# A two-layer hybrid trunk on one core: the transposes of v are asked for one projection later, and the delta branch's z projections are made beside the block inversion and parked in DRAM

## The chip, the cores and the metric

The kernel is written for one core of a Trainium2 chip. The core has four compute engines that run side by side, each through an instruction stream of its own: TensorE (PE: matmuls and transposes, results in PSUM banks), VectorE (DVE), ScalarE (ACT: activations and copies) and GpSimd (POOL). SyncE (SP) issues DMA transfers, and here so does ACT. The engines meet at semaphores. The metric is the device time of one execution in microseconds, lower is better; the time before is the median of three runs.

## What is computed

Two layers of a trunk over 512 latent tokens and 256 context tokens of width 1024. Each layer normalizes and modulates its input (shift, scale and gate come from a projection of a conditioning vector, the "ada" product), projects it by `w_in`, runs three branches of width 512 and merges them by gates:

```python
h = rms_norm(x, norm_g) * (1.0 + scale) + shift          # shift, scale, gate: silu(c) @ w_ada + b_ada
conv_val, conv_glu, conv_z, dq, dk, dv, dz, dbeta, ddecay, aq, ak, av, az, mgate = split(h @ w_in)
# delta branch: short convolution and silu of q, k, v; q and k l2-normalized; beta, g from dbeta, ddecay
sol = triangular_solve(a, rhs)                            # a = strict(k_beta k^T * decay) + I, per chunk
S   = S * exp(g_last) + (k * exp(g_last - g))^T v_new     # scan over chunks, forward and backward
y_delta = rms_norm(o_forward + o_backward, dn_norm_g) * silu(dz)
# conv branch: depthwise convolution over 31 tokens of val * sigmoid(glu), layer norm, silu, * silu(z)
# attention branch: difference of two softmaxes, 4 heads, keys over latent and context tokens, * silu(az)
x = x + gate * (sum over branches of sigmoid(mgate) * (y @ w_branch)) @ w_out
```

The first layer carries 768 tokens through everything (`TOK`); the second needs only 512 (`SEQ`) wherever the context's result is not read again.

## The kernel before

**Weights and products.** A weight unit is 128 x 1024 floats, 512 KB. It is streamed by an SP DMA into one of four `raw` buffers, ACT copies it to its rounded high part `wH` (L751), POOL subtracts to get the low part `wL` (L1676), and PE's `dense` (L418) makes three passes (high x high, low x high, high x low): 48 matmuls for 768 tokens, 24 for 512. `ahead(u)` prepares weights up to three units on. An "ada" unit is different work on the same stream: 16 small matmuls (L509) and a few tiny DVE operations (L1219, L1222).

**The order of work.** `schedule()` writes one list of items by hand, `ITEMS`, and every engine walks that list and does its own part of each item in order. Nothing is reordered at run time: an engine that waits inside one item holds back its part of all later ones. PSUM is handed out in four slots in rotation (`product`).

**The delta branch.** For each of four heads there are three projections, items `dqkv` of kind dk, dv and dq. On each, ACT copies the product into a padded tile (`pad`, L883), DVE makes the short convolution (L1356), ACT applies silu (L896, L897). In the dv item PE then transposes silu's result `vb` (`vturn`, by `turn`, L442) and ACT copies it to `Vtm` (L901); this is all inside the item dv. After it the item `dsum` of the previous head makes the sums of squares on PE (L434), from which ACT computes a reciprocal root in four steps (Ln and Exp, a table load before each, L757 and L760). After the heads come the projections val, glu of the conv branch (`glu` items) and `leaf` items, in which DVE eliminates 32 x 32 blocks (L1422, L1426), then the block inversion: `five`, `fiveb`, `six`, `sixb`, short PE steps with copies by DVE and ACT between them. Then the `scan` over chunks, and `dout` for each head: the z projection (unit dz), POOL's squares `dosq` (L1758), their sum on PE, ACT's silu of z (L1014) and reciprocal root, and DVE's `don` (L1525) and `y32` (L1532). While these run, and long after, DVE makes the 31 taps of the conv branch (L1270, L1274), a few of them at a time; `merge_steps(l, 1)` is the merge of that delta branch (its gates and its output projections).

**Ada units.** Layer 0's list holds 32 ada units that are not needed at once. Twelve (`early`) stand around the inversion of layer 0, three before `five`, three before `fiveb`, three before `six`, three before `sixb`. The other twenty (`late`) are woven at even distances into `mid`, the items of attention and of the merges in layer 0.

## Time and profile before

| | |
|---|---|
| median of three runs | 2379.46 us (2377.32 to 2382.97) |
| the profiled execution: own time | 2383.71 us |
| its span, first to last instruction | 2381.9 us |
| mean granted TensorE clock | 0.887 of full speed |
| busy: PE, DVE, ACT, POOL | 1942.8, 1073.2, 982.3, 818.1 us |

The trace is of the one profiled execution. The shares are averages over stages that have different limits, so a stage is read by itself: which engine is busy through it, and what the others wait for. The stages lie as follows in the span. Layer 0: heads of the delta branch 106 to 288 us, glu and leaf 288 to 388, inversion 388 to 442, scan to 501, dout to 568, the conv phase to about 700, attention 701 to 1203 (first head to 948), merge to 1318. Layer 1: heads 1425 to 1598, leaf 1633 to 1682, inversion 1682 to 1703, scan to 1752, dout and the conv phase to 1894, attention and the end from there.

### The profile page before, as it was taken

What the parts mean: (1) busy time and instruction counts of PE and PEld (TensorE: products, weight loads), DVE (VectorE), ACT (ScalarE), POOL (GpSimd) and SP (SyncE); (2) the same over time, 40 slices, a digit from 0 to 9 for tenths busy, and PEclk for the clock granted to TensorE, in tenths of its full rate; (3) what the DMA queues carried; (4) which work ended last, traced back from release to release, by engine and by line L of the source; (5) the groups of instructions that cost most, each with busy time, mean ns of one, the idle gap of its engine ahead of it and who ended that gap; (6) DMA issues with size and microseconds to landing.
All of it is one profiled execution on the core that took longest, in us unless ns stands there. A gap on an engine that the chain in (4) does not pass through costs nothing. (4 is left out here: it accounts for less than half of the span.)

```text
span 2381.9 us, 28536 instructions
## 1 busy us (share of the span) xinstructions
PE 1942.8 (82%) x11444; PEld 1620.6 (68%) x11444; DVE 1073.2 (45%) x1592; ACT 982.3 (41%) x1318; POOL 818.1 (34%) x428
## 2 busy tenths in 40 slices
PE   7677896999779998878789867676688599888697
PEld 6666785987658887666577746565677387666476
DVE  3444656459960232423401234557769803334302
ACT  4345542243124344544532144564343245455521
POOL 0122323544534534232134211233245454322152
PEclk8588995899889999988899888898799799999898
DMA  4221221411101221111112312122112122101023
GB/s 173 73 76 55 68 84 63 136 51 60 47 27 63 71 71 54 54 36 45 36 53 97 113 47 72 58 72 75 44 65 80 35 83 69 62 27 33 30 82 113
DMA packets 66195, 157.95 MB, mean 66 GB/s; under 512 B 5329, under 2 KB 28177, under 8 KB 65809
## 3 DMA queue, kind: packets, MB, share of 16 engines
q1 hardware_dynamic: 33264, 122.46, 15.9%
q10 hardware_dynamic: 32800, 33.66, 4.4%
q8 instruction: 93, 1.52, 0.3%
q14 instruction: 38, 0.30, 0.0%
HBM read 145.52 MB, written 10.58 MB: 66 GB/s over the span
## 5 line engine op out<-in xcount | busy, mean ns | idle before, releaser
L1676 POOL TENSOR_TENSOR wL<-raw,wH 128x1024 fp32r<-128x1024 f32 x210 | 565.0, 2693 | 1123.0 <-ACT wH L751 1122.8
L418 PE MATMUL banks<-hH,wH 128*128 128x512 f32 x1984 | 598.3, 363 | 75.3 <-issue 32.9
L418 PE MATMUL banks<-hL,wH 128*128 128x512 f32 x1984 | 583.0, 356 | 0.0
L418 PE MATMUL banks<-hH,wL 128*128 128x512 f32 x1984 | 581.1, 355 | 0.0
L418 PEld LDWEIGHTS banks<-hH,wH 128*128 128x128 f32 x1984 | 328.4, 192 | 140.3 <-issue 74.7
L751 ACT ACTIVATE wH<-raw 128x1024 fp32r<-128x1024 f32 x226 | 237.4, 1053 | 396.7 <-DMA raw<-wstream 396.4
L418 PEld LDWEIGHTS banks<-hL,wH 128*128 128x128 f32 x1984 | 327.1, 192 | 56.6 <-issue 3.4
L418 PEld LDWEIGHTS banks<-hH,wL 128*128 128x128 f32 x1984 | 326.1, 192 | 55.0
L1274 DVE SCALAR_TENSOR_TENSOR acc<-padc,vecs,acc 128x783 f32<-128x783 f32 (+1 forms) x240 | 263.8, 1170 | 0.0
L418 PE MATMUL banks<-yH,wH 128*128 128x512 f32 (+1 forms) x288 | 94.8, 384 | 51.5 <-DVE mT L1565 19.2
L509 PE MATMUL banks<-wH,csx 128*128 128x128 f32 x384 | 122.2, 343 | 13.1 <-DVE wL L1209 13.0
L1565 DVE TENSOR_TENSOR gm<-banks,sg 128x768 f32<-128x768 f32 (+1 forms) x32 | 26.4, 825 | 210.9 <-PE banks L418 147.1
L774 ACT ACTIVATE Pa<-banks,stat 128x768 f32<-128x768 f32 (+1 forms) x80 | 64.5, 811 | 137.0 <-DVE stat L1235 136.7
L509 PE MATMUL banks<-wL,csx 128*128 128x128 f32 x384 | 120.2, 338 | 0.0
L1039 ACT ACTIVATE sg<-banks 128x768 f32<-128x768 f32 (+1 forms) x48 | 33.8, 705 | 198.0 <-DVE mT L1565 115.3
L509 PEld LDWEIGHTS banks<-wH,csx 128*128 128x128 f32 x384 | 97.0, 253 | 16.1 <-issue 14.9
L509 PEld LDWEIGHTS banks<-wL,csx 128*128 128x128 f32 x384 | 97.9, 255 | 0.3 <-issue 0.2
L418 PEld LDWEIGHTS banks<-yH,wH 128*128 128x128 f32 x288 | 51.2, 203 | 64.0 <-issue 35.4
L418 PE MATMUL banks<-yL,wH 128*128 128x512 f32 (+1 forms) x288 | 91.5, 373 | 0.0
L418 PE MATMUL banks<-yH,wL 128*128 128x512 f32 (+1 forms) x288 | 91.0, 371 | 0.0
L757 ACT ACT_TABLE_LOAD x52 | 66.7, 1283 | 56.3 <-PE banks L434 55.4
L465 PE MATMUL banks<-kh,qh 64*128 64x256 f32 (+1 forms) x288 | 64.2, 564 | 30.8 <-ACT vr L1152 19.9
(249 smaller groups left out, 2607.0 us busy)
## 6 DMA issues: line engine op xcount, KB each, us to landing
raw<-wstream SPq DMA_DIRECT2D x226, 512.0 KB, 3.5
E<-g_rows ACTq DMA_DIRECT2D x16, 384.0 KB, 6.9
egb<-eg_rows ACTq DMA_DIRECT2D x20, 256.0 KB, 4.0
inb<-intra_rows ACTq DMA_DIRECT2D x20, 256.0 KB, 4.2
xs<-xT SPq DMA_DIRECT2D x1, 3072.0 KB, 16.1
intra_rows<-E ACTq DMA_DIRECT2D x8, 384.0 KB, 3.3
xs<-xT ACTq DMA_DIRECT2D x1, 3072.0 KB, 10.6
x_between<-xs ACTq DMA_DIRECT2D x8, 384.0 KB, 3.4
```

The lines of the kernel that those rows point to most:

```text
L418: last = pe.matmul(out[:, a:b], w, m[:, kt, a:b], start=(kt == 0 and j == 0), stop=(kt == kts - 1 and j == 2))
L465: last = pe.matmul(outs[m][:, o:o + b - a], q_[r, qt * P:(qt + 1) * P], k_[r, a:b], start=True, stop=True)
L509: last = pe.matmul(out[:, 0:P], csx[:, 4 * kt:4 * kt + P], w[i][:, kt * P:(kt + 1) * P], start=(kt == 0 and j == 0), stop=(kt == KT - 1 an ...
L751: act.activation(wH[w % RING][:, :], raw[w % RING][:, :], ACT.Copy).then_inc(*tick("act", "hi", v))
L757: ins = act.activation(dst[:, 0:n], place[readkey][:, 0:n], ACT.Ln, bias=e, scale=scale)
L774: act.activation(Pa[i][m][:, 0:w], place[key][:, 0:w], ACT.Exp, bias=stat[:, i, 2 + m:3 + m], accum_out=stat[:, i, 4 + m:5 + m]).then_inc( ...
L1039: act.activation(sg[d % 2][:, 0:n], place[u][:, 0:n], ACT.Sigmoid).then_inc(*tick_read("act", u))
L1274: ins = dve.scalar_tensor_tensor(acc[:, t, 0:W], padc[:, t, k:k + W], w, acc[:, t, 0:W], ALU.mult, ALU.add)
L1565: dve.tensor_tensor(dst, place[(u, j)][:, 0:n], sg[j][:, 0:n], ALU.mult).then_inc(*tick_read("dve", (u, j)))
L1676: pool.tensor_tensor(wL[w % RING][:, :], raw[w % RING][:, :], wH[w % RING][:, :].bitcast(F32), ALU.subtract).then_inc(*tick("pool", "lo", v))
```

## The change

Four things are done.

1. `vturn` and ACT's copy to `Vtm` leave the item dv and become an item of their own, `vt`, which stands after the next head's dk projection (for the last head, after the first glu item).
2. The z projections leave `dout` and become items `dz`: head 0's before the last leaf item, head 1's between `five` and `fiveb`, head 2's between `fiveb` and `six`, head 3's between `six` and `sixb`. ACT applies silu into `gl[h % 2]` and issues a DMA to a DRAM tensor `zscr`; in `dout` a DMA `z_in` brings each back, and DVE's `y32` waits for it instead of for the silu. ACT and DVE wait for the last two of the writes before the scan begins.
3. All 32 ada units of layer 0 are now `late`, woven into `mid`; none stands around the inversion.
4. Two gate projections of the delta branch's merge move up, between `dout` 0 and 1 and between 1 and 2. Semaphores are made only if they are used.

```diff
--- before.py
+++ after.py
@@ -97,7 +97,7 @@
             out.append(("dqkv", l, h, "dk"))
-            out += [("dsq", l, h - 1)] * (h > 0)
+            out += [("vt", l, h - 1), ("dsq", l, h - 1)] * (h > 0)
             out.append(("dqkv", l, h, "dv"))
@@ -106,14 +106,14 @@
         late = [("ada", 0, m) for m in range(16, 24)] + [("ada", 1, m) for m in range(24)] if l == 0 else []
-        early, late = late[:12], late[12:]
-        out += [("dsq", l, NT - 1), glu[0], ("dsum", l, NT - 1), glu[1], ("dturn", l, NT - 1), ("kq", l, NT - 1)]
-        out += leaf[:3] + [glu[2]] + leaf[3:6] + [glu[3]] + leaf[6:]
-        out += early[:3] + [("five", l)] + early[3:6] + [("fiveb", l)] + early[6:9]
-        out += [("six", l, 1), ("six", l, 0)] + early[9:] + [("sixb", l, 1), ("sixb", l, 0)]
+        dz = [("dz", l, h) for h in range(NT)]
+        out += [("dsq", l, NT - 1), glu[0], ("vt", l, NT - 1), ("dsum", l, NT - 1), glu[1], ("dturn", l, NT - 1),
+                ("kq", l, NT - 1)]
+        out += leaf[:3] + [glu[2]] + leaf[3:6] + [glu[3]] + leaf[6:7] + [dz[0]] + leaf[7:]
+        out += [("five", l), dz[1], ("fiveb", l), dz[2], ("six", l, 1), ("six", l, 0), dz[3], ("sixb", l, 1), ("sixb", l, 0)]
         out += [("scan", l, s) for s in range(NC)]
-        out += [("dout", l, h) for h in range(NT)]
-        out += merge_steps(l, 1)
+        out += [("dout", l, 0), ("gate", l, 1, 0), ("dout", l, 1), ("gate", l, 1, 1), ("dout", l, 2), ("dout", l, 3)]
+        out += merge_steps(l, 1)[2:]
         out += [("ln", l)]
@@ -142,7 +142,7 @@
         return [("av", l, item[2])]
-    if k == "dout":
+    if k == "dz":
         return [("dz", l, item[2])]
@@ -188,9 +188,11 @@
         names += ["w_high", "w_low_pool", "w_low_dve", "raw0", "raw1", "raw2", "raw3", "small_in", "x_in", "x_out", "rope_in"]
-        names += ["g_out", "eg_out", "e_in0", "e_in1", "i_out0", "i_out1"]
+        names += ["g_out", "eg_out", "e_in0", "e_in1", "i_out0", "i_out1", "z_out0", "z_out1", "z_in0", "z_in1"]
         names += ["%s_in%d%d" % (n, d, i) for n in ("eg", "intra") for d in range(2) for i in range(2)]
-        sem = {n: ctx.enter_context(nc.semaphore(n)) for n in names}
+        used = {n for n, _ in steps.values()} or {names[0]}
+        made = {n: ctx.enter_context(nc.semaphore(n)) for n in names if n in used}
+        sem = {n: made.get(n, next(iter(made.values()))) for n in names}
         count = {n: 0 for n in sem}
@@ -534,8 +537,9 @@
                     unit((kind, l, h), kind)
-                    if kind == "dv":
-                        turn(("vturn", l, h), vb[h % 2], TOK, ("silu", "dv", l, h))
+                elif k == "vt":
+                    h = it[2]
+                    turn(("vturn", l, h), vb[h % 2], TOK, ("silu", "dv", l, h))
                 elif k == "dsum":
@@ -646,10 +650,11 @@
                             last.then_inc(*tick("pe", "pe", ("O", l, s, d)))
+                elif k == "dz":
+                    unit(("dz", l, it[2]), "dz")
                 elif k == "dout":
                     n = ntok(l, "dz")
-                    unit(("dz", l, h), "dz")
                     allsum(it, ones[:, :], lambda t, a, b: do[h % 2][:, a:b], n, lambda t: ("dosq", l, h), 1)
@@ -779,6 +784,11 @@
                         *tick("e_in%d" % (h % 2), "Ein", l, h, d, by=16))
+
+            def z_in(l, h):
+
+                n = ntok(l, "dz")
+                act.dma_start(do[4 + h % 2][:, 0:n], zscr[:, h, 0:n]).then_inc(*tick("z_in%d" % (h % 2), "zin", l, h, by=16))
@@ -895,11 +905,12 @@
                     act.activation(dst[:, 0:SEQ], c3[i][:, 0:SEQ], ACT.Silu).then_inc(*tick("act", "silu", kind, l, h))
-                    if kind == "dv":
-                        key = ("vturn", l, h)
-                        act.wait_ge(*done("pe", key))
-                        act.activation(Vtm[:, :, h, :], place[key][:, 0:TOK].rearrange("p (c e) -> p c e", c=NC),
-                                            ACT.Copy).then_inc(*tick_read("act", key))
+                elif k == "vt":
+                    h = it[2]
+                    key = ("vturn", l, h)
+                    act.wait_ge(*done("pe", key))
+                    act.activation(Vtm[:, :, h, :], place[key][:, 0:TOK].rearrange("p (c e) -> p c e", c=NC),
+                                   ACT.Copy).then_inc(*tick_read("act", key))
                 elif k == "dsum":
@@ -982,6 +993,8 @@
                     if g == 0:
+                        act.wait_ge(*done("zout", l, 2))
+                        act.wait_ge(*done("zout", l, 3))
                         scan_in(l, 0)
@@ -998,20 +1011,30 @@
                         scan_in(l, s + 2)
-                elif k == "dout":
+                elif k == "dz":
                     h = it[2]
                     act.wait_ge(*done("pe", u))
-                    act.wait_ge(*done("S", l, NC, 1))
+                    act.wait_ge(*(done("zout", l, h - 2) if h >= 2 else done("glu", l, 2 + h)))
+                    act.activation(gl[h % 2][:, 0:n], place[u][:, 0:n], ACT.Silu).then_inc(*tick_read("act", u))
+                    act.wait_ge(*done("read", u, 0))
+                    act.dma_start(zscr[:, h, 0:n], gl[h % 2][:, 0:n]).then_inc(*tick("z_out%d" % (h % 2), "zout", l, h, by=16))
+                elif k == "dout":
+                    h = it[2]
+                    n = ntok(l, "dz")
                     if h == 0:
+                        act.wait_ge(*done("S", l, NC, 1))
                         act.wait_ge(*done("oT", l, NC - 1, 0))
                         act.dma_start(cs[:, :, :], rope).then_inc(*tick("rope_in", "rope_in", l, by=16))
-                    if h >= 2:
-                        act.wait_ge(*done("y32", 1, l, h - 2))
-                    act.activation(do[4 + h % 2][:, 0:n], place[u][:, 0:n], ACT.Silu).then_inc(*tick_read("act", u))
+                        z_in(l, 0)
+                        z_in(l, 1)
+                    else:
+                        act.wait_ge(*done("y32", 1, l, h - 1))
+                        if h + 1 < NT:
+                            z_in(l, h + 1)
                     rsqrt(None, do[2 + h % 2], 1.0 / P, eps, ("dors", l, h), it, n)
@@ -1480,6 +1503,9 @@
                         dve.wait_ge(*done("negeg", l))
+                        if s == 0:
+                            dve.wait_ge(*done("zout", l, 2))
+                            dve.wait_ge(*done("zout", l, 3))
                         if s:
@@ -1525,7 +1551,7 @@
                     dve.wait_ge(*done("don", l, h))
-                    dve.wait_ge(*done("read", ("dz", l, h), 0))
+                    dve.wait_ge(*done("zin", l, h))
                     if h >= 2:
@@ -1756,8 +1782,9 @@
                     pool.tensor_tensor(do[h % 2][:, 0:n], oT[:, h, 0:n], oT[:, h, 0:n], ALU.mult).then_inc(*tick("pool", "dosq", l, h))
+                    lowy(1, l, h, n, do[6 + h % 2])
+                elif k == "dz":
                     ahead(units_of(it)[0])
-                    lowy(1, l, h, n, do[6 + h % 2])
                 elif k == "glu":
```

**Place 1, ACT, the third head's v in layer 0.** `vb` is silu's result, `Vtm` its transposed copy, `rsd` the reciprocal roots of the head before, `kT` silu of k, `pad` the next product's copy. Before:

```order
L884 ACTIVATE pad_1_92<-banks 128x512
L896 ACTIVATE vb_95<-c_1_94 128x256
L897 ACTIVATE vb_95<-c_1_94 128x512
L901 ACTIVATE Vtm<-banks 128x6x128
L757 ACT_TABLE_LOAD
L757 ACTIVATE rsd_99<-banks,misc 128x768
L760 ACT_TABLE_LOAD
L760 ACTIVATE rsd_99<-rsd_99 128x768
```

After (L901 is now L912, L757 is L762, L751 is L756):

```order
L906 ACT_TABLE_LOAD
L906 ACTIVATE kT<-c_0_93 128x256
L907 ACTIVATE kT<-c_0_93 128x512
L912 ACTIVATE Vtm<-banks 128x6x128
L756 ACTIVATE wH_58<-raw_54 128x1024
L893 ACTIVATE pad_1_92<-banks 128x256
L894 ACTIVATE pad_1_92<-banks 128x512
L906 ACTIVATE vb_95<-c_1_94 128x256
L907 ACTIVATE vb_95<-c_1_94 128x512
L762 ACT_TABLE_LOAD
L762 ACTIVATE rsd_99<-banks,misc 128x768
```

What moved: the copy to `Vtm`, which stood between silu of v and the first table load, is gone from there; the one in the rows of after is the second head's, behind the third head's silu of k, and silu of v is followed by the reciprocal root at once.

**Place 2, ACT, the inversion of layer 1.** `T1a`, `T1b`, `PT`, `PM` are tiles of the inversion, `gl` takes silu of glu or of z, `dz_rows` is the DRAM tensor. Before:

```order
L1029 ACTIVATE gl_112<-banks 128x512
L944 ACTIVATE T1a<-banks 128x768
L949 ACTIVATE PT_115<-CPT 32x24x32 x2
L955 ACTIVATE PM<-banks 32x24x32 x2
L961 ACTIVATE PT_115<-banks 32x24x32
L967 ACTIVATE PM<-CP 32x24x32 x4
L973 ACTIVATE T1b<-banks 128x768 x2
```

After:

```order
L955 ACTIVATE T1a<-banks 128x768
L960 ACTIVATE PT_115<-CPT 32x24x32 x2
L756 ACTIVATE wH_57<-raw_53 128x1024
L1021 ACTIVATE gl_112<-banks 128x512
L1023 DMA dz_rows<-gl_112 128x512
L966 ACTIVATE PM<-banks 32x24x32 x2
L972 ACTIVATE PT_115<-banks 32x24x32
L978 ACTIVATE PM<-CP 32x24x32 x4
L756 ACTIVATE wH_58<-raw_54 128x1024
L1021 ACTIVATE gl_111<-banks 128x512
L1023 DMA dz_rows<-gl_111 128x512
L984 ACTIVATE T1b<-banks 128x768 x2
```

What moved: between the copies of the inversion there now stand the silu of z and a DMA out for each of heads 1 to 3, each behind its unit on PE, and the weights' copies (L756) for them.

**Place 3, POOL, dout of layer 1.** `do<-oT` is `dosq`, the squares that the reciprocal root of a head starts from; `yL` is the low part of a head's result, `wL` of a weight unit. Before:

```order
L1758 TENSOR_TENSOR do_143<-oT 128x512
L1676 TENSOR_TENSOR wL_60<-raw_52,wH_56 128x1024
L1682 TENSOR_TENSOR yL<-do_149,yH 128x512
L1758 TENSOR_TENSOR do_144<-oT 128x512
L1676 TENSOR_TENSOR wL_61<-raw_53,wH_57 128x1024
L1682 TENSOR_TENSOR yL<-do_150,yH 128x512
L1758 TENSOR_TENSOR do_143<-oT 128x512
L1676 TENSOR_TENSOR wL_62<-raw_54,wH_58 128x1024
```

After:

```order
L1784 TENSOR_TENSOR do_143<-oT 128x512
L1708 TENSOR_TENSOR yL<-do_149,yH 128x512
L1702 TENSOR_TENSOR wL_60<-raw_52,wH_56 128x1024
L1784 TENSOR_TENSOR do_144<-oT 128x512
L1708 TENSOR_TENSOR yL<-do_150,yH 128x512
L1702 TENSOR_TENSOR wL_61<-raw_53,wH_57 128x1024
L1784 TENSOR_TENSOR do_143<-oT 128x512
L1708 TENSOR_TENSOR yL<-do_149,yH 128x512
L1784 TENSOR_TENSOR do_144<-oT 128x512
```

What moved: heads 1 and 2 have a weight unit (of a gate projection) ahead of their squares, where it stood behind them, and head 3 has none; the units of z are gone from here.

## Rows read from the trace of the kernel before

**Rows 1.** The profile's page: busy time by engine; the chain that ended last, by engine.

```profile
PE 1942.8 (82%) x11444; PEld 1620.6 (68%) x11444; DVE 1073.2 (45%) x1592; ACT 982.3 (41%) x1318; POOL 818.1 (34%) x428
...
PE 18%; DVE 10%; issue 3%; ACT 3%; POOL 0%; DMA 0%; ACTq 0%; DVEq 0%; POOLq 0%
```

**Rows 2.** Stages: from, to, length, busy of PE, PEld, DVE, ACT, POOL, clock.

```profile
106.00:288.00 182.00, 141.25 (x775) 120.42 (x776) 81.71 (x113) 97.10 (x124) 45.48 (x35) 0.87 0.21 64
...
388.00:442.00 54.00, 47.30 (x809) 45.38 (x802) 14.98 (x37) 22.62 (x32) 21.95 (x11) 0.59 0.28 90
...
701.00:948.00 247.00, 241.02 (x1387) 204.11 (x1386) 53.74 (x86) 108.42 (x136) 113.36 (x58) 0.99 0.20 62
948.00:1203.00 255.00, 203.61 (x1120) 161.17 (x1119) 90.86 (x178) 121.34 (x181) 65.41 (x32) 0.88 0.14 44
...
1425.00:1598.00 173.00, 128.59 (x669) 107.15 (x670) 79.79 (x113) 93.00 (x117) 42.86 (x34) 0.86 0.23 65
...
1633.00:1682.00 49.00, 18.65 (x110) 15.22 (x112) 46.84 (x68) 8.25 (x10) 11.50 (x5) 0.72 0.17 52
1682.00:1703.00 21.00, 16.42 (x664) 15.83 (x656) 10.45 (x15) 11.00 (x14) 0.99 (x2) 0.59 0.02 4
...
1766.00:1894.00 128.00, 88.66 (x348) 69.12 (x349) 126.97 (x138) 40.10 (x46) 70.34 (x22) 0.85 0.19 61
```

**Rows 3.** Groups by line, 106 to 288 us: busy, mean ns, idle before them.

```profile
L442 PE MATMUL banks<-cons,vb 128*128 128x128 f32 x24 | 6.1, 425 | 40.7 <-ACT vb L897 40.7
```

**Rows 4.** Timeline of ACT, layer 0, heads 1 and 3: start, length, [idle before].

```profile
185.66 0.81 ACT L901 ACTIVATE Vtm<-banks 128x768 f32<-128x768 f32 x1 [1.69 <-PE banks L442]
186.49 1.28 ACT L757 ACT_TABLE_LOAD   x1
...
273.10 0.81 ACT L901 ACTIVATE Vtm<-banks 128x768 f32<-128x768 f32 x1 [1.69 <-PE banks L442]
275.70 1.28 ACT L757 ACT_TABLE_LOAD   x1 [1.79 <-PE banks L434]
```

**Rows 5.** Timelines of POOL and DVE in the leaf of layer 0.

```profile
366.81 7.91 POOL L1676 TENSOR_TENSOR wL<-raw,wH 128x1024 fp32r<-128x1024 f32 x3 [4.89 <-ACT wH L751]
...
366.57 0.62 DVE L1426 TENSOR_TENSOR M<-M,tmp 128x440 f32<-128x440 f32 x1
367.22 2.64 DVE L1422 TENSOR_TENSOR tmp<-M 128x420 f32<-128x420 f32 x1
```

**Rows 6.** DVE in layer 0's inversion; two units from the chain of waits.

```profile
403.69 0.22 DVE L1219 TENSOR_SCALAR ada<-banks,vecs 128x2 f32<-128x2 f32 x1 [3.39 <-PE banks L491]
...
1965.53 5.47 PE banks L418 x24
...
2049.41 7.97 PE banks L418 x24
```

**Rows 7.** DMA issues of the page: the nearest to z's, with median time to landing.

```profile
x_between<-xs ACTq DMA_DIRECT2D x8, 384.0 KB, 3.4
```

**Rows 8.** Timelines at dout's first head: DVE twice, POOL; the page's group of taps.

```profile
516.43 1.02 DVE L1525 SCALAR_TENSOR_TENSOR do<-oT,vecs,do 128x768 f32<-128x768 f32 x1 [14.71 <-ACT do L760]
...
1764.13 0.75 DVE L1525 SCALAR_TENSOR_TENSOR do<-oT,vecs,do 128x512 f32<-128x512 f32 x1 [11.04 <-ACT do L760]
...
1753.23 1.04 POOL L1758 TENSOR_TENSOR do<-oT 128x512 f32<-128x512 f32 x1 [5.22 <-DVE oT L1516]
...
L1274 DVE SCALAR_TENSOR_TENSOR acc<-padc,vecs,acc 128x783 f32<-128x783 f32 (+1 forms) x240 | 263.8, 1170 | 0.0
```

**Rows 9.** 701 to 1318 us: ada's matmuls; timelines of PE and DVE between.

```profile
L509 PE MATMUL banks<-wH,csx 128*128 128x128 f32 x160 | 39.0, 286 | 0.0
...
955.82 2.93 PE L465 MATMUL banks<-kh,qh 64*128 64x512 f32 x8 [5.14 <-ACT vr L1152]
...
1113.24 0.66 PE L442 MATMUL banks<-cons,Pa 128*128 128x128 f32 x2 [5.71 <-DVE Pa L1251]
...
1003.97 2.33 DVE L1248 TENSOR_SCALAR Pa<-Pa,c 128x768 f32<-128x768 f32 x1
```

More of the change, by code:

```diff
@@ L341, in build @@
         egscr = nc.dram_tensor("eg_rows", (2, NC, NT, P), F32, kind="Internal").ap()
+        zscr = nc.dram_tensor("dz_rows", (P, NT, TOK), F32, kind="Internal").ap()
         iscr = nc.dram_tensor("intra_rows", (2, NC, P, NT, P), F32, kind="Internal").ap()
```

## The prediction, made blind

> **What bounds the kernel now.** I began with the page: PE is busy 82% of the span, but only 18% of the chain that ended last is PE's and 10% DVE's [rows 1], so no engine bounds it throughout, and I went on by stages [rows 2]. The reader is to see four kinds. In the heads of the delta branch (106 to 288 us) PE is busy 141 of 182 us, and nearly all of its idle time, 40.7 us, stands before the transposes of v, which wait for ACT's silu [rows 3]. ACT's own timeline tells why PE's idle time isn't simply there to be had [rows 4]: ACT waits for DVE's convolution, makes silu of v, waits 1.69 us for the transposes, copies 0.81, and in head 3 waits 1.79 more for the sums of squares, which PE makes behind the transposes. ACT and DVE hand each projection back and forth, and PE waits for that pair. In the inversion PE is busy 47.3 of 54 us in layer 0, with nine ada units in the stretch, at a granted clock of 0.59, but 16.4 of 21 us in layer 1, where none stand. In the leaf of layer 1 DVE is the bound (46.8 of 49 us) and PE is idle for 30. From 1766 to 1894 DVE is the bound too, busy 127 of 128. Attention in layer 0 is PE-bound in its first part (241 of 247 us) and a mixture later (204 of 255).
>
> **Transposes of v later.** The instructions are the same in number. What goes is ACT's two waits: 1.69 + 1.79 = 3.5 us in heads 2 and 3. In head 1 the table load follows the copy at once, so only 1.69 and some contention of the sums go, taken as 2.0; for head 0 I take 3.0, between 1.7 and 3.5. The copy of 0.81 is not saved, it is made later without a wait, after a unit of PE. Layer 0: 3.0 + 2.0 + 3.5 + 3.5 = 12.0. Layer 1: 1.7 + 2.0 + 3.5 + 3.0, less 0.8 for the last head's copy, which now stands among the glu items: 9.4. Together **-21.4**, with bounds of -14 (only the 1.69 in each of the eight heads) and -83, twice the 40.7 of [rows 3], if the heads became PE-bound. I stay near the lower end: with the transposes out of its way PE arrives early at the next thing that ACT or DVE owes it, the normalized k, and waits there.
>
> **The leaf.** DVE's eliminations take 0.62 us, and 2.64 where a `wL` subtraction of POOL runs [rows 5]: 2.0 us lost for each. Layer 0 loses three ada units from the leaf and gains dz 0: -4.1. Layer 1 gains one: **+2.0**. The unit itself runs in PE's idle time. Here the Trainium skill bears on the case (SBUF — State Buffer, section SBUF: two separate sides): VectorE operations with two SBUF inputs and GpSimd operations share a port pair that is locked for a whole instruction. By that rule, the trace agrees, 2.64 against 0.62.
>
> **The inversion.** Layer 1 shows the bare chain of 21 us, 4.6 of it idle on PE [rows 2]. A unit of 24 matmuls takes 5.47 us, one after an idle stretch 7.97, so the low clock costs 2.5 [rows 6]. Three units dz 1 to 3 are 16.4 us, plus 2.5 once, less some 2 of idle time filled, plus 0.5 for the wait for the writes to DRAM before the scan: **+17.4**. In layer 0 units have 768 tokens, 1.5 x 5.47 = 8.2, taken as 8.5 a unit: 21 + 25.5 + 2.5 - 2 + 0.5 = 47.5 in the place of 54, **-6.5**. That the ada units are dear here is seen in DVE's timeline, where they come 3.8 us apart (3.39 + 0.22 + 0.16) [rows 6]; in attention 16 matmuls go at 286 ns [rows 9], about 2.1 us for a unit. The wait for the writes: a transfer of 384 KB lands after 3.4 us [rows 7], while `sixb` and its copies take some 3; bounds 0 and +3.4 a layer. The Trainium skill (TensorE: Matmul & The Clock Gate, section What's actually happening) has the clock low after idleness and high again once the engine has been kept busy. The row of layer 0's inversion, 0.59 while 47.3 of 54 us are recorded busy, speaks against leaning on it. Were all three units of layer 1 at the low clock, the stage would pay 3 x 2.5 instead of 2.5, +22.4 in place of +17.4; if the clock came back at once, +15.
>
> **dout.** The first head's DVE operation comes 14.7 us after the scan in layer 0 and 11.0 in layer 1 [rows 8], since the sum of squares is queued behind the z unit and ACT makes silu first. Without them: in layer 1 squares 1.04, sum 1.0, two table loads and two activations 3.9, so 6.0: -5.0; in layer 0 by 768 tokens 7.5: -7.2. Then the conv phase, which DVE bounds: POOL loses three `wL` beside DVE, 3 x 2.05 = -6.2 in each layer. Against that the gate units stand ahead of the squares of heads 1 and 2 (place 3). From `y32` of a head to `don` of the next the chain is then copy 0.6, `yL` 1.5, `wL` 2.8, squares 1.5, sum 1.5, root 4.4, some 12 us, and DVE has six taps, at a mean of 1.17 us [rows 8] and with a `wL` beside them 8 to 10 us, to fill it: +2.5 to 3 of idle time for two heads and less for the third, +7.5 and +7. Layer 0 **-5.9**, layer 1 **-4.2**; bounds -13 and 0 each. z comes back in 3.4 us beside that chain and is hidden; if it weren't, DVE would wait at the first `y32`.
>
> **Twelve more ada units in attention.** By the order, 4 of the 12 fall into the first part, 3 into head 1's, 2 each into heads 2's and 3's, 1 into the merge. The first part is PE-bound, 4 x 2.1 less a little, 7.5. In head 1's part one new unit stands right before the 5.14 us in which PE waits for ACT, in head 2's one before the 5.71 us wait for DVE's `Pa` [rows 9], and in head 3's one before a similar wait; these are absorbed. The others' PE time is about 3.5, 0.5, 0.5 and 2. Each also brings a copy of 1.05 to ACT and a `wL` to POOL that holds DVE: `Pa` scaled in 2.33 us beside one [rows 9]. For that I add 3. Sum **+17**, bounds +8 (only the first part) and +30 (12 x 2.5).
>
> **The sum.** Layer 0: -12.0 - 4.1 - 6.5 - 5.9 + 17 = -11.5. Layer 1: -9.4 + 2.0 + 17.4 - 4.2 = +5.8. Together -5.7 us on the profiled execution's 2383.7, so 2378.0 for it; that execution lies 4.25 above the median of 2379.46, so a median of 2373.8. The change is one of large terms that nearly cancel: 21 us from the transposes and 22 from the rest against 36.
>
> **The rivals.** First, the added ada units cost in full: in the later heads PE waits for DVE's `Pa` chain, each added `wL` holds that chain for 2.0 us where PE has room, and where DVE has room PE pays 2.1. For it speaks the 2.33 us row; against it that POOL's subtraction meets such an operation only sometimes. 12 units at 2.1, plus a share that pays both, is +28: 2385. It decides from 2.3 us a unit on, where the sum becomes slower by more than 0.2%; chance 0.22. Second, more of the PE time is recovered than I grant, the ada units mostly hidden (+10) and the heads giving -27: 2361; for it speaks that 51 us of the 255 are idle, against it the heads' ACT chain; 0.18. Third, the detour through DRAM becomes the new wait: 3.4 us before the scan and 2 at the first `y32`, in both layers, +9: 2382; against it, z is issued long before; 0.08. Fourth, the change does little to the heads, since ACT's waits return as waits for DVE's convolution, and only 8 of the 21 us come: 2387; 0.07. My forecast keeps 0.45, its own range 2366 to 2380.
>
> **How the numbers follow.** About 0.2%, 4.8 us, is what a measurement here can tell from no change: faster is below 2374.7, slower above 2384.2. Of my forecast's 0.45 I put 0.28 faster and 0.17 same; the second rival is faster, 0.18; the third gives 0.06 same and 0.02 slower; the first 0.05 same and 0.17 slower; the fourth slower, 0.07. Faster 0.46, same 0.28, slower 0.26. The range reaches to the second rival's middle and past the first's: 2360 to 2389.
>
> **What would show it.** In the trace after: ACT's table load directly behind silu of v, and the heads of layer 0 shorter by 12 us and layer 1's by 9; PE's idle time there not gone but standing before transposes of k or the products with it; `sixb` in layer 1 later by 17 and the stage's clock higher; dout's first operation 5 to 7 us sooner, with new idle time on DVE before heads 1 and 2; attention of layer 0 longer by some 14 us and its merge by 2. Wrong it would be if ada units cost over 2.3 us each, if the heads stay as long, or if the z units find PE at the low clock throughout.

## The result and the profile after

The changed kernel takes 2391.46 us (median of 9 runs, 2383.95 to 2396.72) where the kernel before takes 2377.32 on the same chip (9 runs): 1.0058 of it, with a 95% interval of 1.0043 to 1.0073. It is 14 us slower; the forecast was 6 us faster, with a range that ended at 2389. Both kernels were run once more in traced executions, so stages can be read twice on either side. Measured from the end of one item to the end of another on PE, in us:

| stage | before, two traces | after, two traces | difference | forecast |
|---|---|---|---|---|
| layer 0: first dk to `five` (heads, glu, leaf) | 266.6, 268.4 | 250.2, 249.9 | -17.5 | -16.1 |
| inversion, to `sixb` | 48.7, 45.7 | 42.7, 42.8 | -4.4 | -7.0 |
| first scan step | 14.3, 13.3 | 17.7, 16.4 | +3.2 | +0.5 |
| dout, conv phase, ln | 200.6, 201.5 | 195.5, 197.4 | -4.6 | -5.9 |
| attention, from z's last to `aout` of head 3 | 468.3, 468.1 | 485.5, 486.3 | +17.7 | +15 |
| merge of the attention branch | 98.4, 97.9 | 100.5, 101.9 | +3.0 | +2 |
| layer 1: first dk to `five` | 240.6, 241.4 | 235.6, 236.8 | -4.8 | -7.4 |
| inversion | 18.2, 18.1 | 34.8, 33.9 | +16.2 | +16.9 |
| first scan step | 6.5, 6.5 | 9.9, 10.4 | +3.6 | +0.5 |
| dout, conv phase, ln | 149.6, 149.1 | 151.2, 148.1 | +0.3 | -4.2 |

The differences add up to +12.8, the forecasts to -5.7. The stages not listed differ no more between the kernels than between two traces of one kernel (there the work ahead of the first dk by 2 us, the output of layer 0 by 2.4, the attention of layer 1 by 3.3 and 5.0).

What the transposes did is seen in ACT's timeline of layer 0, in head 3: start, length, what, idle before. The copy to `Vtm` is head 2's.

```profile
251.70 0.61 ACT L907 ACTIVATE kT<-c 128x512 f32<-128x512 f32 x1
252.22 0.79 ACT L912 ACTIVATE Vtm<-banks 128x768 f32<-128x768 f32 x1
...
259.33 0.62 ACT L907 ACTIVATE vb<-c 128x512 f32<-128x512 f32 x1
259.96 1.28 ACT L762 ACT_TABLE_LOAD   x1
```

The copy has no idle time before it and the table load follows silu directly; of the waits in [rows 4] both are gone. Of PE's 40.7 us of idle time in these heads [rows 3] 25.2 are left, and 21.5 of them stand before the sums of squares and the transposes of k (by line, 104 to 272 us):

```profile
L437 PE MATMUL banks<-sqd,ones 128*128 128x512 f32 (+1 forms) x24 | 11.6, 624 | 11.6 <-POOL sqd L1740 11.6
...
L445 PE MATMUL banks<-cons,kT 128*128 128x128 f32 x18 | 4.5, 425 | 9.9 <-DVE kT L1387 9.9
```

The inversion of layer 1 stands in the chain of waits, with a z unit (L421) between its steps:

```profile
1671.43 7.07 PE banks L421 x24
1678.50 1.75 PE banks L584 x114
1680.25 0.32 PE banks L591 x17
1680.57 3.96 issue
1684.53 2.29 PE banks L591 x78
1686.83 7.84 PE banks L421 x24
1694.66 2.94 PE banks L605 x96
1697.61 5.67 PE banks L421 x24
```

Two of the three units take 7.07 and 7.84 us, one 5.67. The 3.96 us are no wait for a copy: they stand inside `fiveb`, within the 96 matmuls of L591 (18 before, 78 behind), where the program has no wait, and the profile names nothing that ended them. The second trace has 3.83 us at the same place, and the kernel before has shorter breaks in the same item (its L580 and L587 are L584 and L591 of after). What causes them stays open. After, and then before:

```profile
1680.10 0.47 PE L591 MATMUL banks<-T1a,CP 32*32 32x32 f32 x18
1684.53 2.29 PE L591 MATMUL banks<-T1a,CP 32*32 32x32 f32 x78 [3.96 <-issue]
...
1685.60 2.16 PE L580 MATMUL banks<-CP,T1a 32*32 32x32 f32 x131 [1.20 <-ACT T1a L944]
1689.30 0.98 PE L580 MATMUL banks<-CP,T1a 32*32 32x32 f32 x57 [1.54 <-issue]
...
1692.65 1.00 PE L587 MATMUL banks<-T1a,CP 32*32 32x32 f32 x29 [0.59 <-issue]
1694.89 4.93 PE L601 MATMUL banks<-PT,PM 64*64 64x64 f32 x96 [1.24 <-DVE PT L1464]
```

By stages (columns as in [rows 2]): layer 0's inversion and scan start, layer 1's inversion, and its dout.

```profile
368.00:415.40 47.40, 43.23 (x817) 38.21 (x818) 10.85 (x16) 16.31 (x20) 8.11 (x5) 0.83 0.17 52
415.40:433.10 17.70, 12.52 (x82) 12.09 (x83) 6.54 (x14) 3.05 (x9) 7.06 (x6) 0.81 0.42 142
...
1666.90:1706.20 39.30, 33.90 (x745) 28.78 (x745) 10.51 (x14) 15.66 (x19) 8.10 (x5) 0.82 0.19 53
...
1759.30:1798.60 39.30, 18.89 (x57) 11.53 (x56) 26.10 (x25) 19.21 (x21) 15.59 (x9) 0.72 0.20 67
```

The granted clock of the inversions rose from 0.59 [rows 2] to 0.83 and 0.82 (in the second trace of before it is 0.63 and 0.71, from `five` to `sixb`), while in dout PE, busy 18.9 of 39.3 us, is at 0.72. DVE has 13 us of idle time in those 39. It had 12 in the same stage before, but there 11.04 of them stood ahead of the first head; now 5.41 do, and the rest stands between the heads.

### The profile page after: what moved, and what is told of

The parts are those of the page before. It is cut to its first block and busy times, and to the rows that moved or that the text cites. A ratio compares the mean times of both kernels' runs of the same rounds, so it can differ in the third digit from the quotient of the medians.

```text
span 2388.7 us, 28558 instructions
## 1 busy us (share of the span) xinstructions
PE 1950.3 (82%) x11444; PEld 1622.0 (68%) x11444; DVE 1063.9 (45%) x1592; ACT 979.0 (41%) x1316; POOL 811.6 (34%) x428
## 5 line engine op out<-in xcount | busy, mean ns | idle before, releaser
L1702 POOL TENSOR_TENSOR wL<-raw,wH 128x1024 fp32r<-128x1024 f32 x210 | 558.2, 2661 | 1152.6 <-ACT wH L756 1152.3
L421 PE MATMUL banks<-hH,wH 128*128 128x512 f32 x1984 | 598.2, 363 | 77.1 <-issue 32.8
L421 PE MATMUL banks<-hH,wL 128*128 128x512 f32 x1984 | 582.3, 355 | 0.0
L421 PE MATMUL banks<-hL,wH 128*128 128x512 f32 x1984 | 582.0, 355 | 0.0
L421 PEld LDWEIGHTS banks<-hH,wH 128*128 128x128 f32 x1984 | 329.0, 193 | 143.0 <-issue 73.4
L756 ACT ACTIVATE wH<-raw 128x1024 fp32r<-128x1024 f32 x226 | 237.6, 1054 | 407.7 <-DMA raw<-wstream 407.5
L421 PEld LDWEIGHTS banks<-hL,wH 128*128 128x128 f32 x1984 | 327.0, 192 | 56.4 <-issue 2.9
L421 PEld LDWEIGHTS banks<-hH,wL 128*128 128x128 f32 x1984 | 325.8, 192 | 53.8
L1297 DVE SCALAR_TENSOR_TENSOR acc<-padc,vecs,acc 128x783 f32<-128x783 f32 (+1 forms) x240 | 251.9, 1118 | 0.0
L421 PE MATMUL banks<-yH,wH 128*128 128x512 f32 (+1 forms) x288 | 96.9, 392 | 65.6 <-issue 35.6
L512 PE MATMUL banks<-wH,csx 128*128 128x128 f32 x384 | 117.0, 333 | 13.4 <-DVE wL L1232 11.4
L512 PE MATMUL banks<-wL,csx 128*128 128x128 f32 x384 | 114.2, 326 | 0.0
L421 PEld LDWEIGHTS banks<-yH,wH 128*128 128x128 f32 x288 | 52.4, 207 | 80.5 <-issue 53.1
L512 PEld LDWEIGHTS banks<-wH,csx 128*128 128x128 f32 x384 | 92.8, 242 | 18.2 <-issue 14.7
L421 PE MATMUL banks<-yL,wH 128*128 128x512 f32 (+1 forms) x288 | 92.6, 377 | 0.0
L421 PE MATMUL banks<-yH,wL 128*128 128x512 f32 (+1 forms) x288 | 92.2, 375 | 0.0
## 6 DMA issues: line engine op xcount, KB each, us to landing
xs<-xT SPq DMA_DIRECT2D x1, 3072.0 KB, 14.3
```

Source lines behind the costliest of these rows:

```text
L421: last = pe.matmul(out[:, a:b], w, m[:, kt, a:b], start=(kt == 0 and j == 0), stop=(kt == kts - 1 and j == 2))
L512: last = pe.matmul(out[:, 0:P], csx[:, 4 * kt:4 * kt + P], w[i][:, kt * P:(kt + 1) * P], start=(kt == 0 and j == 0), stop=(kt == KT - 1 an ...
L756: act.activation(wH[w % RING][:, :], raw[w % RING][:, :], ACT.Copy).then_inc(*tick("act", "hi", v))
L1297: ins = dve.scalar_tensor_tensor(acc[:, t, 0:W], padc[:, t, k:k + W], w, acc[:, t, 0:W], ALU.mult, ALU.add)
L1702: pool.tensor_tensor(wL[w % RING][:, :], raw[w % RING][:, :], wH[w % RING][:, :].bitcast(F32), ALU.subtract).then_inc(*tick("pool", "lo", v))
```

## The experiments

Kernels are compared with before by ratio, since the chips differ by a few us.

**The transposes alone.** Before, with change 1.

```diff
+            out += [("vt", l, h - 1), ("dsq", l, h - 1)] * (h > 0)
...
+        out += [("dsq", l, NT - 1), glu[0], ("vt", l, NT - 1), ("dsum", l, NT - 1), glu[1], ("dturn", l, NT - 1), ("kq", l, NT - 1)]
```

> The transposes of v are asked one projection later, nothing else of the change is made. Theory A (the heads gained what the trace of after shows, and the other parts lost it): the heads of layer 0 are 13 us shorter and those of layer 1 some 8 to 10, so the time is 2354 to 2358 where before is 2377. Theory B (part of that gain belonged to the z units or ada units that left the stages behind it, or is given back later, in the glu and leaf stages): the gain is 5 to 12 us, 2365 to 2372.

Measured: 2358.8 us against 2379.86, 0.9921 (0.9896 to 0.9946): 21 us by the medians, 19 by the ratio. Heads of layer 0, first dk to the first glu item, 166.2 us for 179.7 and 181.7; of layer 1 153.8 for 164.6 and 165.6, of which 3 come back in the glu and leaf stages. Theory A, with a little of B in layer 1.

**The ada units alone.** Before, with `early` left empty.

```diff
-        early, late = late[:12], late[12:]
+        early = []
```

> Only the twelve ada units of layer 0 move from around the inversion into attention and the merges; z stays in dout, the transposes stay where they were. Theory A (an ada unit costs in attention what the trace of after shows, 19 us for twelve, and is dear at the inversion, 3.8 us for six of them and 2.1 for three, 6 us more through three subtractions beside the leaf): attention +19, inversion and leaf -35, so 16 us faster, about 2361. Theory B (in attention they cost as much as they save, since each brings a copy and a subtraction to engines that PE waits for): within 5 us of before.

Measured: 2363.08 against 2379.86, 0.993 (0.991 to 0.995), 17 us faster. `five` to `sixb` of layer 0 falls from 48.7 and 45.7 to 18.0 us, the stage from behind the first glu item to `five` by 7.5, attention rises by 18.2, the merge by 3.3. Theory A. Of the loss of the change nothing is due to this part.

**The z units alone.** The changed kernel with the ada units, the transposes and the gates where they were.

```diff
-        out += [("five", l), dz[1], ("fiveb", l), dz[2], ("six", l, 1), ("six", l, 0), dz[3], ("sixb", l, 1), ("sixb", l, 0)]
+        out += [("five", l)] + early[3:6] + [dz[1], ("fiveb", l)] + early[6:9] + [dz[2], ("six", l, 1), ("six", l, 0)]
+        out += early[9:] + [dz[3], ("sixb", l, 1), ("sixb", l, 0)]
...
+        out += [("dout", l, h) for h in range(NT)]
```

> Only the z units move (beside the leaf and the inversion, parked in DRAM); the ada units stay around the inversion, the transposes and the gates stay where they were. Theory A (the three z units of the inversion lie on the path in both layers, the scan's loads are held back by the wait for the writes, and the conv phase, which DVE bounds, gives back only the first head's wait and the subtractions): layer 0 +25 in the inversion, +2 in the leaf, +3.4 at the scan, -11 at dout; layer 1 +16.6, +2, +3.4, -9: together +32, about 2409. Theory B (the forecast's prices, with the scan's wait at 0.5 and dout's gain in full): +20 to +25. Theory C (the z units are mostly hidden, and the loss in the change came from the ada units): within 8 us of before.

Measured: 2425.07 against 2379.86, 1.0189 (1.0167 to 1.0211), 45 us slower, more than theory A. Inversion +27 in layer 0 and +17.9 in layer 1, scan start +2.5 and +1.7, and from dout through ln only -4.1 and -1.4, where A had -11 and -9. Why it gives so little back is in POOL's, PE's and DVE's rows of its dout in layer 1:

```profile
1804.04 1.49 POOL L1786 TENSOR_TENSOR do<-oT 128x512 f32<-128x512 f32 x1
...
1805.67 2.04 PE L439 MATMUL banks<-do,ones 128*128 128x512 f32 x2 [7.80 <-POOL do L1786]
...
1802.88 4.53 DVE L1299 SCALAR_TENSOR_TENSOR acc<-padc,vecs,acc 128x512 f32<-128x512 f32 x4
1810.42 0.75 DVE L1553 SCALAR_TENSOR_TENSOR do<-oT,vecs,do 128x512 f32<-128x512 f32 x1 [3.01 <-ACT do L767]
```

DVE's four taps take 4.53 us, no longer slowed by a `wL` (6.63 before), and then DVE waits 3.01 us for the root of the next head. Its squares could not be made before the low part of the head before, and the sum of them takes PE, now idle ahead of it, 2.04 us.

**Before, traced again.**

> The kernel before once more, for a second trace of it. If the stages up to the first projection of layer 0 differ by some 3 us from the first trace and all later ones by under 0.5, the difference between the traces that stands ahead of the change is chance.

Its span is 2378.4 us (the first trace 2381.9), 2 us less up to the first dk, and single stages differ by up to 6, not by under 0.5 (attention's head 2 90.2 for 94.1, the conv phase of layer 1 77.7 for 84.0, taken back in ln). It is those sums of stages that agree, and differences of under 2 us in one stage say nothing.

**Transposes and ada units, z left in dout.** The first two edits together.

> The transposes of v one projection later and the twelve ada units moved into attention; the z units stay in dout, silu at hand, no DRAM. Theory A (the parts add up, and the z move alone makes the change slow): -21 and -17 as each measured alone, so 38 us faster than before, 2339 to 2343. Theory B (the two gains share waits, or the ada units only pay because z takes their place): 20 to 30 us faster.

Measured: 2352.49 against 2381.55, 0.9873 (0.9838 to 0.9908): 30 us by the ratio, at the upper end of theory B, with 22 to 39 us inside the interval, so theory A's 38 isn't excluded. Either way, the change without its z units is faster than before, not slower.

**Gates behind dout.**

```diff
-        out += [("dout", l, 0), ("gate", l, 1, 0), ("dout", l, 1), ("gate", l, 1, 1), ("dout", l, 2), ("dout", l, 3)]
-        out += merge_steps(l, 1)[2:]
+        out += [("dout", l, h) for h in range(NT)]
+        out += merge_steps(l, 1)
```

> The changed kernel with the two gate projections back behind the four dout items. Theory A (the stage totals of the traces: moving the gates up trades idle time in dout for fewer subtractions in the conv phase): layer 0 slower by 1, layer 1 faster by 3, together within 3 us of the changed kernel, 2388 to 2392. Theory B (the forecast's: a subtraction ahead of the squares costs DVE 2.5 to 3 us for each of the two heads, in both layers): 10 us faster than the changed kernel, 2381.

Measured: 1.0061 (1.0039 to 1.0082), the same as the change. Theory A: dout is 5.7 us shorter in both layers, and the phase behind it, through ln, gives back 6 to 7 in layer 0 and 1 to 5 in layer 1.

**The z unit of head 3 beside that of head 2.**

```diff
-        out += [("five", l), dz[1], ("fiveb", l), dz[2], ("six", l, 1), ("six", l, 0), dz[3], ("sixb", l, 1), ("sixb", l, 0)]
+        out += [("five", l), dz[1], ("fiveb", l), dz[2], dz[3], ("six", l, 1), ("six", l, 0), ("sixb", l, 1), ("sixb", l, 0)]
```

> The changed kernel with the z unit of head 3 right behind that of head 2, so that its write to DRAM lands before the inversion ends. Theory A (the scan starts late because its loads are issued behind the wait for that write, 3.4 us in each layer): the first scan step begins 3.4 us sooner after the inversion in both layers, 7 us faster than the changed kernel, 2384. Theory B (the loads wait for something else, or the unit costs more where it stands now): no faster than 2389.

Measured: 1.0019 (0.9999 to 1.0039), so 10 us better than the kernel above by the ratio, and 7 to 9 better than the change. Scan starts of 15.2 and 6.5 us, for 17.7 and 9.9 in the change (16.4 and 10.4 in its second trace). Theory A in layer 1, where 6.5 is the time of before; in layer 0 only 1.2 to 2.6 us of the 3.4 come, and 15.2 is still above the 14.3 and 13.3 of before. ACT's timeline of the change at the end of layer 0's inversion shows the queue:

```profile
413.27 0.33 ACTq L1023 DMA_DIRECT2D dz_rows<-gl  x1
...
415.38 0.81 ACT L991 ACTIVATE PM<-banks 64x768 f32<-64x768 f32 x1 [0.59 <-PE banks L620]
417.42 0.33 ACTq L801 DMA_DIRECT2D egb<-eg_rows  x1
```

and here, with the unit moved:

```profile
416.88 0.81 ACT L991 ACTIVATE PM<-banks 64x768 f32<-64x768 f32 x1 [0.59 <-PE banks L620]
417.12 0.33 ACTq L801 DMA_DIRECT2D egb<-eg_rows  x1
```

The load is issued 2.0 us after the last copy begins in the change (417.42 - 415.38), 0.2 here.

**All z units before the last leaf item.**

```diff
-        out += leaf[:3] + [glu[2]] + leaf[3:6] + [glu[3]] + leaf[6:7] + [dz[0]] + leaf[7:]
-        out += [("five", l), dz[1], ("fiveb", l), dz[2], ("six", l, 1), ("six", l, 0), dz[3], ("sixb", l, 1), ("sixb", l, 0)]
+        out += leaf[:3] + [glu[2]] + leaf[3:6] + [glu[3]] + leaf[6:7] + dz + leaf[7:]
+        out += [("five", l), ("fiveb", l), ("six", l, 1), ("six", l, 0), ("sixb", l, 1), ("sixb", l, 0)]
```

> The changed kernel with all four z units before the last leaf item, none in the inversion. Theory A (the units lie on the path in the inversion and are hidden where PE waits for DVE's elimination): layer 1, where PE is idle for 28 us, -16.6 in the inversion, +6 in the leaf for three more subtractions, -3.4 at the scan; layer 0, where only some 10 us are free, -24.6, +17 and -3.4; together 25 us faster than the changed kernel, 2366. Theory B (the subtractions and the units stretch the leaf as much as the inversion gains): 5 us faster or less.

Measured: 2365.87 against 2381.55, 0.9934 (0.9913 to 0.9955), 29 us less than the change by the ratio. Inversions of 19.8 and 17.0 us for 42.7 and 34.8, the stages to `five` longer by 9.8 of 63.3 (behind glu 1) in layer 0 and by 4.7 in layer 1. Theory A: in the leaf most of the three units is hidden, in the inversion little.

**Squares one head early.** Three kernels with this edit on POOL and the gates behind dout: on the last kernel, on the change, and on the one with z in dout.

```diff
+                    for q in ((0, 1) if h == 0 else (h + 1,) if h + 1 < NT else ()):
...
+                        pool.tensor_tensor(do[q % 2][:, 0:n], oT[:, q, 0:n], oT[:, q, 0:n], ALU.mult).then_inc(*tick("pool", "dosq", l, q))
                     lowy(1, l, h, n, do[6 + h % 2])
```

> As the kernel with all four z units before the last leaf item, with two more changes: POOL makes the squares of a head's output one head early, ahead of the low part of the head before, and the gate projections stand behind dout again. Theory A (what the z move should give back in dout is lost in a chain: copy of one head's result on ACT, low part and squares of the next on POOL, their sum on PE, which stands idle and is at the low clock, and the root on ACT; DVE waits 3.0 to 4.4 us a head for it where its taps are no longer slowed): with the squares early the wait before the heads 1 to 3 falls below 1 us, dout and the conv phase are 8 us shorter in each layer, 16 us faster than the kernel without it, 2350. Theory B (DVE's taps and subtractions set the phase, the idle time is made up elsewhere): no more than 4 us faster.

> The changed kernel with the squares one head early and the gate projections behind dout; the z units stay in the inversion. Theory A: 16 us faster than the changed kernel with the gates behind dout, some 2377, which is the time of before: the change is then repaid in dout but not won. Theory B: within 4 us of the changed kernel.

> The transposes and the ada units moved, z in dout, squares one head early. Theory A (with z in dout DVE waits only 0.9 us for the same chain, since its taps are slowed by the z weights' subtractions and the sums find PE warm): at most 3 us faster than without, that is 2341 to 2353. Theory B (the chain costs the same wherever z stands): 10 us or more.

Measured, against 2383.13: 2330.71, 0.9778 (0.9748 to 0.9809); 2359.21, 0.9898 (0.9882 to 0.9914); 2342.99, 0.9818 (0.978 to 0.9855). So 37, 39 and 13 us better than without the edit (the first also has the gates back behind dout, an edit that alone made no difference on the change). For the first two theory A holds for the mechanism and underrates the size. In the second, from dout to ln layer 0 takes 181.4 us for 196.9 with the gates behind and layer 1 137.3 for 146.6, 25 us of the 39; the rest I can't place, since it lies in stages that the edit leaves alone (4.4 in attention's head 2, which takes 92 to 98 us in the traces with the moved ada units). DVE in layer 1 of the second of these kernels:

```profile
1741.91 0.75 DVE L1551 SCALAR_TENSOR_TENSOR do<-oT,vecs,do 128x512 f32<-128x512 f32 x1 [5.59 <-ACT do L765]
...
1748.67 0.74 DVE L1551 SCALAR_TENSOR_TENSOR do<-oT,vecs,do 128x512 f32<-128x512 f32 x1
...
1755.83 0.74 DVE L1551 SCALAR_TENSOR_TENSOR do<-oT,vecs,do 128x512 f32<-128x512 f32 x1
...
1762.23 0.74 DVE L1551 SCALAR_TENSOR_TENSOR do<-oT,vecs,do 128x512 f32<-128x512 f32 x1
```

and in the change:

```profile
1765.45 0.75 DVE L1551 SCALAR_TENSOR_TENSOR do<-oT,vecs,do 128x512 f32<-128x512 f32 x1 [5.41 <-ACT do L765]
1778.06 0.75 DVE L1551 SCALAR_TENSOR_TENSOR do<-oT,vecs,do 128x512 f32<-128x512 f32 x1 [3.68 <-ACT do L765]
1791.08 0.75 DVE L1551 SCALAR_TENSOR_TENSOR do<-oT,vecs,do 128x512 f32<-128x512 f32 x1 [3.68 <-ACT do L765]
1802.67 0.75 DVE L1551 SCALAR_TENSOR_TENSOR do<-oT,vecs,do 128x512 f32<-128x512 f32 x1 [4.35 <-ACT do L765]
```

Heads follow at 6.4 to 7.2 us there and at 11.6 to 13.0 here (9.9 to 11.6 with the gates behind and the squares late). With z in dout the 13 us by the ratio decide nothing: the intervals with and without the edit overlap, and the traces show a gain of 4.8 us from dout to ln in layer 0 (195.4 for 200.2) and none in layer 1 (149.9 for 149.1), near the 3 of theory A.

**The change again.**

> The changed kernel once more, on the same chip as the three others, for a second trace of it and as their yardstick. Its time against before is to be 1.004 to 1.007 of it; stages that differ from its first trace by over 2 us are not to be read as effects anywhere.

Measured: 1.0049 (1.0029 to 1.0069).

**Ada units put before waits.**

```diff
+            at = mid.index(("pv", l, h, 4)) if l == 0 else None
...
+                mid = [it for i, it in enumerate(mid[:at]) if i not in near] + units + mid[at:]
```

> As the kernel with z before the last leaf item and the squares first, with one more change: in each of the attention heads 1 to 3 the two ada units ahead of the transposes of the fifth query tile are put directly before these, where PE waited 6.2 us (head 1), 5.7 (head 2) and 2.3 (head 3) for DVE's Pa in the trace of before. Theory A (PE time that is idle in a wait is free for a unit that needs nothing from the chain that is waited for, and the forecast only misjudged which units fall into waits): 4 us less in heads 1 and 2 each, 2 in head 3, 8 to 10 us faster than the kernel it is made from. Theory B (a unit costs its 2.1 us wherever it stands, since each takes a PSUM slot of the rotation and holds later products back, and each brings a subtraction beside DVE): within 3 us.

> The kernel that the one above is made from, once more on the same chip, as its yardstick: 0.975 to 0.981 of the time of before.

Measured: 0.9782 (0.9756 to 0.9807), its yardstick 0.9807 (0.9782 to 0.9832): 6 us faster, between the theories, and the intervals overlap. In the trace heads 1 to 3 are 2.1, 1.3 and 0.9 us longer, not shorter, than in the trace of the kernel it is made from; differences of that size say little. The experiment doesn't decide between the theories.

## Why the prediction was wrong

The sum was off by 18.5 us. By the table, the wait before the scan is 5.8 of it, dout with the conv phase 5.8, the ada units 3.7, the inversion of layer 0 and the stages to `five` of layer 1 2.6 each; the two others were 2.1 better than forecast. Two sums of the prediction are slightly off and change nothing: twice 40.7 is 81.4, not 83, and the rest that gains is 20.7, not 22.

**The heads** were right: -21.4 against 19 to 21 us for the transposes alone. PE's idle time there fell by 15.5 us in layer 0, about what the stage became shorter, and what is left moved to the sums and to k's transposes, as [rows 3] and the rows of after show.

**The leaf and the inversion.** The leaf of layer 0 gave the 4.1 us; in layer 1, dz 0 costs 3.5 to 3.8 us there (against the kernels without it), not 2.0. The inversion of layer 0 was 2.6 us too hopeful: its units take 10.8, 10.4 and 8.7 us, 29.9 and not 28. That of layer 1 was right in sum, +16.9 against +16.2, and partly by luck. Its units take 20.6 us where I had 18.9, and the break in `fiveb` is 3.96 us for 1.54 + 0.59. Against that the short steps between them run faster than before, which I had at nothing: the 96 matmuls of L605 take 2.94 us, those of L601 before took 4.93 (4.39 in its second trace), at a granted clock of 0.82 for 0.59. Of idle time the units fill the 1.20 and 1.24 us in which PE waited for copies, near the 2 that I took. The Trainium skill (TensorE: Matmul & The Clock Gate, section What's actually happening) has the clock low after idleness and high once the engine has been kept busy. The trace agrees as far as it goes: the units lie between the prediction's two rows of 5.47 and 7.97 us, and more than one of them pays.

**The wait before the scan** failed: "plus 0.5 for the wait for the writes", with a bound of 3.4, where the stages are 3.2 and 3.6 us longer. I priced only how long the write is out. What I left out is what is queued behind the waiting ACT, the eight loads of the scan, whose own transfers then start late: in layer 0 the write landed at 417.3, the first load was issued at 417.42, and PE waited 5.18 us for what it carried, instead of 1.98 in the trace of before (last row):

```profile
422.50 3.96 PE L636 MATMUL banks<-egb,S 128*128 128x128 f32 x16 [5.18 <-POOL egb L1769]
...
445.85 3.49 PE L632 MATMUL banks<-egb,S 128*128 128x128 f32 x16 [1.98 <-POOL egb L1743]
```

In layer 1 the move of head 3's unit removed it whole, and every kernel here without a write at that place has 6.5 us, those with it have 7.8 to 10.4. In layer 0 the kernels without it lie at 13.2 to 16.4 us and those with it at 16.3 to 17.7, so there the wait is some 2 us of the 3.2; what else moves that stage isn't shown.

**dout and the conv phase** failed as much, "Layer 0 -5.9, layer 1 -4.2", measured -4.6 and +0.3. The first head came as forecast: DVE's wait before it fell from 14.71 to 6.42 us in layer 0 and from 11.04 to 5.41 in layer 1. The step that failed is the idle time between the heads, "+2.5 to 3 of idle time for two heads and less for the third, +7.5 and +7". It is 4.40, 4.39 and 4.79 us in layer 0, 3.68, 3.68 and 4.35 in layer 1. Before, 1.36 and 0.92 us stood there in all, so the term is +12.2 and +10.8. For the first two heads of layer 1 the chain has the 12 us that I gave it and the taps are still slowed, six in 7.95 us, since the subtraction of a gate unit runs beside them where z's did; the two waits are some 1 us each above my price. The third, for which I took less, waits longest: nothing slows its taps any more, six take 5.85 us instead of 7.99, while its chain is only some 1.4 us shorter. There what the missing subtraction gives and the idle time are the same time, and I had counted the gain without the loss. Nor had I seen that PE, with no units between, makes the sums of heads 2 and 3 in 2.04 and 2.05 us, where they took 1.10 before. DVE in layer 1; the first two rows are of before:

```profile
1773.99 0.75 DVE L1525 SCALAR_TENSOR_TENSOR do<-oT,vecs,do 128x512 f32<-128x512 f32 x1 [0.92 <-ACT do L760]
...
1784.73 7.99 DVE L1274 SCALAR_TENSOR_TENSOR acc<-padc,vecs,acc 128x512 f32<-128x512 f32 x6
...
1766.23 0.69 DVE L1558 TENSOR_TENSOR do<-do,do 128x512 f32<-128x512 f32 x1
...
1779.45 7.95 DVE L1297 SCALAR_TENSOR_TENSOR acc<-padc,vecs,acc 128x512 f32<-128x512 f32 x6
...
1792.47 5.85 DVE L1297 SCALAR_TENSOR_TENSOR acc<-padc,vecs,acc 128x512 f32<-128x512 f32 x6
```

The kernels with the squares first show what this hides, 15.5 and 9.3 us in the two layers. What bounded was the chain through POOL's queue, not the detour of z through DRAM: `y32` (L1558) waits for z and starts 0.03 us after `don` in every head. The third rival, DRAM, was right for the scan and wrong for dout.

**The ada units** in attention cost 17.7 + 3.0, not 17; per unit 1.7 us. The sum hides two errors: the first part rose by 1.8 us, not 7.5, and heads 1 to 3 by 16, not 4.5 (beside the 3 for all that a unit brings). "These are absorbed" failed. In the trace of after the new unit before head 1's first scores doesn't fall into the wait for ACT; it takes one of the four PSUM slots, and the scores themselves now wait, so that they begin 4.79 us after it:

```profile
928.50 5.65 PE L468 MATMUL banks<-kh,qh 64*128 64x512 f32 x16 [4.79 <-issue]
```

In [rows 9] only the second of the two groups had waited, and from the end of the item before to the end of these scores there pass 12.3 us instead of 9.5. That a slot is the cause is read from the order of the slots, not shown by a run. The first rival, 2.3 us and more for each unit, fell for the twelve together; in heads 1 to 3, where seven of them cost 16 us, its price was right.

**The balance.** The first two parts of the change are worth about 30 us together, and the z units cost some 44 where the change puts them: 45 when moved alone. With z before the last leaf item and the squares first the same ideas give 0.9778 of before, and 0.9807 when measured again: about 2% faster, the fastest kernel here beside the one with the ada units before waits.

## What to carry to other kernels

A stage in which one engine is busy 99% may be so because another slows it; before taking that slowing away, add up the chain that runs beside it, step by step with its queues, since it becomes the bound at once, and what goes into waiting for it is no gain. A wait is priced by what is queued behind it on its engine, here eight DMA issues, and not only by how long the awaited thing is out. A unit fits into PE's idle time where that time is one long wait, 28 us in the leaf; among short steps that depend on each other most of it lies on the path. That a buffer in rotation can put it there even right before a wait is likely here, but not shown.

## What the runs showed of the hardware

Writes of z to DRAM took longer than the transfers I priced them by, 3.4 us for 384 KB: the medians are 4.4 for 384 KB and 5.3 for 256 KB. Each of them, in both layers, ran beside a weight transfer of 512 KB, so that doesn't tell why the smaller ones take longer. Of these the one in the leaf landed after 3.5 us and the three in the inversion after 5.0 to 5.6; the cause stays open.

```profile
dz_rows<-gl ACTq DMA_DIRECT2D x4, 384.0 KB, 4.4
do<-dz_rows ACTq DMA_DIRECT2D x4, 384.0 KB, 4.7
dz_rows<-gl ACTq DMA_DIRECT2D x4, 256.0 KB, 5.3
```
